# Feed-forward stages of a two-block transformer kernel: 54 pairs of output tiles as seven half-size products, down projection in three parts

## The chip, the cores and the metric

The kernel runs on one core of a Trainium2 chip. The metric is the device time in microseconds (us) of one execution; lower is better. The time before is the median of three runs.

## The reference, cut to what matters

Two blocks of two layers each act on a sequence of 512 rows and 1024 columns, all in float32. Each of the four layers ends in a feed-forward stage with 2816 inner columns. In the first block (layers 0 and 1 here):

```python
h2 = modulate(rms_norm(x, norm2_g), shift2, scale2)
u, g = jnp.split(h2 @ w_up, 2, axis=-1)
u = causal_dwconv(u, w_conv, b_conv)      # 3 taps along the sequence
y = (jax.nn.silu(u) * g) @ w_down
x = x + gate2[:, None, :] * y
```

In the second block (layers 2 and 3 here):

```python
h = rmsnorm(x, norm_ffn[i])
g = h @ w_gate; u = h @ w_up
x = x + (silu(g) * u) @ w_down
```

## The kernel before, in words

All activations lie transposed: columns of the model on the 128 partitions, the 512 rows of the sequence along the free dimension. X is the residual stream in eight such tiles. Every operand of a matmul is held as two float32r parts, high and low (HH and HL for the normed input, FH and FL for the inner activations, hi and lo for weights), and a product of a 128x128 weight block with a 128x512 activation is three matmuls: high with high, high with low, low with high (lines 440 to 442, function dot).

**Weights.** SyncE loads chunks of 512 KB (eight blocks of 128x128) into a ring of six slots, raw. The load of chunk n waits until chunk n-6 has been used up; the waits stand in one queue, in the order of the chunks (sync_program). ScalarE rounds a chunk into hi (line 1371, split), up to four chunks ahead of TensorE, at fixed places of its own program; GpSimd subtracts and writes lo (line 2977, pool_program), in the order of the chunks. VectorE and ScalarE each run one list of steps in order; what stands behind a waiting step waits too.

**A feed-forward stage.** ffn_up computes, for each f of 22, one output tile "up" and one "gateup" (projects, project, tile_of), each eight blocks deep: 24 matmuls 512 columns wide. Output goes to one of four PSUM banks in turn. In layers 0 and 1, ScalarE evicts "up" with the last tap of the convolution (line 1860), VectorE adds the other two taps (2672, 2675), ScalarE applies silu (1863). In layers 2 and 3 VectorE scales by the row roots RW (2665), then silu (1853). When "gateup" is done VectorE multiplies (2655), in layers 2 and 3 scales by RW again (2658), ScalarE writes FH (1849) and VectorE FL (2660). After all 22 tiles, out_proj multiplies FH and FL, 22 blocks deep, by the down weights, for eight tiles d, and VectorE adds them to X (x_update, 2120 and 2122). Some of the last tiles d are done in two halves of 256 rows of the sequence (WHOLE is the number of those done whole), so that the next norm can begin on the first half.

**What is woven in.** In layer 0 the products that make the modulation vectors (ada) are woven between the tiles: at each step that is not BUSY the schedule puts in a piece. Their weights come through the same ring of six slots, and VectorE multiplies and adds them (2291, 2294, 2317, 2321).

## Time and profile before

| | us |
|---|---|
| median of 3 runs | 2902.85 |
| lowest and highest run | 2902.02, 2904.55 |
| span of the profiled execution | 2901.7 |
| TensorE busy, share of the span | 2866.5, 99% |
| VectorE, ScalarE, GpSimd busy | 1115.5, 1075.3, 1171.4 |

The span goes from the first to the last instruction of one execution; the profile has no total for that execution, so its own time is taken as its span, 1.15 us under the median of the runs. In rows of the timeline the first number is the start in us from the span's start, the second the duration; the bracket says how long the engine had been idle and who released it. In rows of the groups, the numbers behind the bar are the busy time in us and the mean duration in ns, then the idle time before them.

### The profile page before, as it was taken

How to read it: one execution, taken by the hardware profiler on the slowest of the kernel's cores; microseconds unless marked ns; L12 is line 12 of the kernel's file. 1: busy time of each engine (PE TensorE's matmuls, PEld its weight loads, DVE VectorE, ACT ScalarE, POOL GpSimd, SP SyncE). 2: the span in 40 equal slices, each digit the busy share in tenths (PEclk: the TensorE clock that was granted, in tenths of full speed). 3: DMA queues.
4: the chain of work that ended last, by engine and by line, in shares of the span. 5: the costliest groups of instructions: out<-in, count | busy, mean ns of one | idle time of the engine just before them, and what ended most of it. 6: DMA issues, size and time to landing. Idle time of an engine off the chain costs nothing.

```text
span 2901.7 us, 33894 instructions
## 1 busy us (share of the span) xinstructions
PE 2866.5 (99%) x14219; PEld 2354.9 (81%) x14219; DVE 1115.5 (38%) x1787; ACT 1075.3 (37%) x1627; POOL 1171.4 (40%) x499
## 2 busy tenths in 40 slices
PE   8999999999999999999999999999999999999999
PEld 5777888888888887788898888888888877788888
DVE  6444572466664534322242211532221256622211
ACT  4335333343332434532343332342222366432322
POOL 2332245344444432344444444444444423344442
PEclk9999999999999999999999999999999999999999
DMA  8331353346554421333333333333333322233332
GB/s 257 103 106 51 106 189 114 90 153 196 195 194 136 115 73 44 88 94 96 101 88 101 95 95 94 96 97 98 94 98 95 105 60 72 77 97 95 98 95 77
DMA packets 507276, 314.04 MB, mean 108 GB/s; under 512 B 14290, under 2 KB 478836, under 8 KB 506868
## 3 DMA queue, kind: packets, MB, share of 16 engines
q1 hardware_dynamic: 507124, 311.87, 36.0%
q8 instruction: 113, 1.85, 0.3%
q14 instruction: 39, 0.32, 0.0%
HBM read 309.73 MB, written 2.10 MB: 107 GB/s over the span
## 4 chain that ended last, share of the span: by engine, by line
PE 95%; DVE 2%; ACT 1%; SPq 1%; DMA 1%; issue 0%; POOL 0%; DVEq 0%; ACTq 0%
PE b L440 22%; PE b L442 21%; PE b L441 21%; PE o L440 6%; PE o L442 6%; PE o L441 6%; PE s L769 1%; DVE aP L2834 1%; PE o L923 1%; PE b L1109 1%; PE b L1111 1%; PE b L1110 1%; PE s L903 1%; PE b L491 0%; PE b L492 0%; PE b L493 0%
## 5 line engine op out<-in xcount | busy, mean ns | idle before, releaser
L2977 POOL TENSOR_TENSOR lo<-raw,hi 128x1024 fp32r<-128x1024 f32 (+2 forms) x489 | 1169.1, 2398 | 1695.8 <-ACT hi L1371 1695.7
L440 PE MATMUL b<-HH,hi 128*128 128x512 f32 x1832 | 726.2, 396 | 1.7 <-DVE X L2120 0.9
L442 PE MATMUL b<-HH,lo 128*128 128x512 f32 x1832 | 713.7, 390 | 0.0
L441 PE MATMUL b<-HL,hi 128*128 128x512 f32 x1832 | 713.6, 390 | 0.0
L1371 ACT ACTIVATE hi<-raw 128x1024 fp32r<-128x1024 f32 (+2 forms) x492 | 506.5, 1035 | 366.8 <-DMA raw<-in_w_down_dram 96.8
L440 PEld LDWEIGHTS b<-HH,hi 128*128 128x128 f32 x1832 | 343.9, 188 | 81.4 <-issue 8.4
L442 PEld LDWEIGHTS b<-HH,lo 128*128 128x128 f32 x1832 | 343.9, 188 | 72.8
L441 PEld LDWEIGHTS b<-HL,hi 128*128 128x128 f32 x1832 | 344.1, 188 | 71.2 <-issue 1.4
L440 PE MATMUL b<-FH,hi 128*128 128x512 f32 (+1 forms) x550 | 207.2, 377 | 0.0
L442 PE MATMUL b<-FH,lo 128*128 128x512 f32 (+1 forms) x550 | 207.0, 376 | 0.0
L441 PE MATMUL b<-FL,hi 128*128 128x512 f32 (+1 forms) x550 | 207.0, 376 | 0.0
L440 PE MATMUL o<-HH,hi 128*128 128x512 f32 x520 | 202.4, 389 | 0.0
L441 PE MATMUL o<-HL,hi 128*128 128x512 f32 x520 | 202.3, 389 | 0.0
L442 PE MATMUL o<-HH,lo 128*128 128x512 f32 x520 | 202.3, 389 | 0.0
L2655 DVE TENSOR_TENSOR CB<-CB,b 128x512 f32<-128x512 f32 x84 | 57.7, 687 | 290.4 <-PE b L442 287.3
L1849 ACT ACTIVATE FH<-CB 128x512 fp32r<-128x512 f32 x88 | 55.6, 632 | 268.1 <-DVE CB L2658 199.2
L2294 DVE SCALAR_TENSOR_TENSOR AA<-raw,CA,AA 128x512 f32<-128x512 f32 x140 | 136.3, 974 | 4.1
L440 PEld LDWEIGHTS b<-FH,hi 128*128 128x128 f32 x550 | 103.5, 188 | 19.0
L441 PEld LDWEIGHTS b<-FL,hi 128*128 128x128 f32 x550 | 103.5, 188 | 18.9
L442 PEld LDWEIGHTS b<-FH,lo 128*128 128x128 f32 x550 | 103.5, 188 | 18.7
L441 PEld LDWEIGHTS o<-HL,hi 128*128 128x128 f32 x520 | 97.6, 188 | 20.3
L442 PEld LDWEIGHTS o<-HH,lo 128*128 128x128 f32 x520 | 97.6, 188 | 20.2
(517 smaller groups left out, 4012.5 us busy)
## 6 DMA issues: line engine op xcount, KB each, us to landing
raw<-in_w_up_dram SPq DMA_DIRECT2D x88, 512.0 KB, 3.9
raw<-in_w_ada_dram SPq DMA_DIRECT2D x80, 512.0 KB, 4.8
raw<-in_w_in_dram SPq DMA_DIRECT2D x76, 512.0 KB, 4.0
raw<-in_w_mg_dram SPq DMA_DIRECT2D x48, 512.0 KB, 3.7
raw<-in_ffn_w_gate_dram SPq DMA_DIRECT2D x44, 512.0 KB, 3.8
raw<-in_ffn_w_up_dram SPq DMA_DIRECT2D x44, 512.0 KB, 3.9
raw<-in_w_down_dram SPq DMA_DIRECT2D x32, 512.0 KB, 3.7
raw<-in_ffn_w_down_dram SPq DMA_DIRECT2D x32, 512.0 KB, 3.6
```

What stands on the lines that cost most here:

```text
L440: e.matmul(out, wh, xh, start=start and k == 0, stop=False)
L441: e.matmul(out, wh, xl, start=False, stop=False)
L442: mm = e.matmul(out, wl, xh, start=False, stop=stop and k == last)
L769: e.matmul(bank[b][:, 0:w], t["rk"][:, h, j * 128:j * 128 + 128], t["rq"][:, h, j * 128:S], start=True, stop=True).then_inc(*m.attn.up(("r ...
L903: e.matmul(o[:, 0:w], t["fq"][:, h, i * 128:w], t["fk"][:, h, 0:w], start=True, stop=False)
L923: mm = e.matmul(bank["o"][:, j * 128:S], t["fv"][:, j, h * 128:h * 128 + 128], t["foxT"][:, c0:c0 + S - 128 * j], start=(j == 0), stop=(j ...
L1109: e.matmul(out[:, :], hi[:, k, :], AH[:, k, :], start=(i == 0), stop=False)
L1371: e.activation(t["hi"][:, c % NSLOT, 0:w], K.raw[:, c % NSLOT, 0:w], ACT.Copy).then_inc(*m.hi.up(c))
L1849: e.activation(t["FH"][:, f, :], CB[:, b, :], ACT.Copy).then_inc(*m.atake.up(("fh", i, f)))
L2294: a = e.scalar_tensor_tensor(out=AA[:, :], in0=raw[:, k * 512:k * 512 + 512], scalar=CA[:, kk:kk + 1], in1=AA[:, :], op0=ALU.mult, op1=ALU ...
L2655: e.tensor_tensor(CB[:, b, :], CB[:, b, :], self.out_of(key)[:, :], ALU.mult).then_inc(*m.vtake.up(key))
L2977: e.tensor_tensor(t["lo"][:, s, 0:w], K.raw[:, s, 0:w], t["hi"][:, s, 0:w].bitcast(F32), ALU.subtract).then_inc(*m.lo.up(n))
```

## The change

For 54 pairs of tiles ("up" f and "gateup" f) the two tiles of eight blocks are computed as seven products of four blocks' depth on 256 columns, after Strassen, in the form with eight sums ahead (Winograd's). 6 pairs are in layer 0 and 16 in each other layer; DIRECT names the f that stay as they were. Per layer, four operands T are made once from HH and HL by twelve VectorE operations of 1024 columns (halves_whole, halves_sums, halves_low) and four of ScalarE (halves_high), in the first four f (HEAD). Per pair, VectorE makes four sums of weight quarters from the raw chunks: sum31 (1024 columns, two sums), sum2 (512, in place in raw), sum4 (512); ScalarE rounds them (pair_high: e31, the chunk nb, e4) and VectorE makes the low parts of e31 (1024) and e4 (512). The low parts of the two chunks na and nb stay with GpSimd; that of na now also waits for sum4. This is done while the tile or pair before is computed. After the products VectorE combines: pair_out row 0 is two operations of 512 columns, row 1 is one more, from copies MP that ScalarE takes of two products in the middle of the pair (pair_copies); two of the seven products overwrite or add to what was copied, and wait for it.

The down projection is done in three parts: blocks 0 to 6 after f = 7, 7 to 13 after f = 14, 14 to 21 at the end by out_proj. FH and FL have eight tiles instead of 22, and VectorE adds to X after each part (down_update, 512 columns). The banks of this stage are six instead of four. In layer 0's and the last layer's down projection WHOLE goes from 7 to 5.

The diff, cut to its core; left out are the names of the new areas, the moved bodies of the tile steps (the same operations under new names ffn_tap, ffn_conv, ffn_silu, ffn_gate, ffn_high, ffn_low) and the rest of the twelve operations for T:

```diff
 BUSY = "busy"
-WHOLE = (8, 5, 7, 5, 8, 8, 8, 8, 7)
...
 BIG4 = ["b0", "b1", "b2", "o"]
+BIG6 = ["b0", "b1", "b2", "o", "s0", "s1"]
+DIRECT = ((*range(9), 10, 11, 13, 14, 15, 17, 19), (0, 1, 2, 3, 11, 18), (0, 1, 2, 3, 11, 18), (0, 1, 2, 3, 11, 18))
+HEAD = 4
+ROOM = 8
+DOWN = {7: (0, 7), 14: (7, 7)}
+LAST = 14
+def ffn_next(i, f):
+    return f + 1 if f + 1 < KF and f + 1 not in DIRECT[i] else None
...
+        self.order = BIG6
+        for f in range(HEAD, KF):
+            if f in DIRECT[i]:
+                for key, ap, c0, freed in jobs(f):
+                    yield from self.project(ap, c0, key, freed)
+            else:
+                yield from self.pair(i, f, up_freed)
+            if f in DOWN:
+                yield from self.down(i, wd, *DOWN[f])
+        self.order = BIG4
+    def half_product(self, out, W, X, start, waits, keys):
+        e, m = self.e, self.m
+        self.q.wait_ge(*waits)
+        (wh, wl), (xh, xl) = W, X
+        for k in range(4):
+            c = slice(128 * k, 128 * k + 128)
+            e.matmul(out, wh[:, c], xh[:, k, :], start=start and k == 0, stop=False, skip_group_check=True)
+            e.matmul(out, wh[:, c], xl[:, k, :], start=False, stop=False, skip_group_check=True)
+            mm = e.matmul(out, wl[:, c], xh[:, k, :], start=False, stop=k == 3, skip_group_check=True)
+        if keys:
+            mm.then_inc(*m.dense.up(*keys))
+    def pair(self, i, f, up_freed):
...
+        K.chunks[na]["above"] = K.chunks[nb]["below"] = (i, f)
+        sa, sb = na % NSLOT, nb % NSLOT
+        hi, lo = t["hi"], t["lo"]
+        EH, EL, _ = K.block(i, f)
+        A11, A12 = [(hi[:, sa, c], lo[:, sa, c]) for c in (slice(0, 512), slice(512, 1024))]
+        s2, A22 = [(hi[:, sb, c], lo[:, sb, c]) for c in (slice(0, 512), slice(512, 1024))]
+        s3, s1, s4 = [(EH[:, u, :], EL[:, u, :]) for u in (*K.ends(na), 2)]
+        T1, T3, T2, T4 = [(t["TH"][:, j, :, :], t["TL"][:, j, :, :]) for j in range(4)]
...
+        bc_, ba, bd = [self.take_bank((x, i, f)) for x in ("up", "mid", "gateup")]
+        C, A, G = self.bank[bc_], self.bank[ba], self.bank[bd]
+        self.half_product(C[:, left], A12, H(1, left), True, [m.lo.at(na), self.free[bc_]], [])
+        self.half_product(A[:, right], s3, T3, True, [m.vtake.at("e31", i, f), m.vtake.at("t", i, 1), self.free[ba]], [])
+        yield BUSY
+        self.half_product(A[:, left], A11, H(0, left), True, [], [("mid", i, f)])
+        self.half_product(G[:, right], s1, T1, True, [m.vtake.at("t", i, 0), self.free[bd]], [("mid5", i, f)])
+        yield BUSY
+        self.half_product(C[:, right], s4, H(1, right), True, [m.vtake.at("e4", i, f)], [("block", i, f)])
+        self.half_product(A[:, left], s2, T2, False, [m.lo.at(nb), m.vtake.at("t", i, 2), m.atake.at("mid", i, f)],
+                          [("up", i, f)])
+        yield BUSY
+        self.half_product(G[:, left], A22, T4, True, [m.vtake.at("t", i, 3), m.atake.at("mid5", i, f)],
+                          [("gateup", i, f), ("chunk", na), ("chunk", nb)])
+        yield BUSY
...
+            if c in K.chunks and K.chunks[c]["split"] and "below" not in K.chunks[c]:
                 w = K.chunks[c]["width"]
...
+    def pair_high(self, i, f, part):
+        EH, _, ER = K.block(i, f)
+        if part == 0:
+            q.wait_ge(m.vtake.at("sum31", i, f))
+            e.activation(EH[:, 0:2, :], ER[:, 0:2, :], ACT.Copy).then_inc(*m.atake.up(("e31", i, f)))
+        elif part == 1:
+            q.wait_ge(m.vtake.at("sum2", i, f))
+            s = (na + 1) % NSLOT
+            e.activation(t["hi"][:, s, :], K.raw[:, s, :], ACT.Copy).then_inc(*m.hi.up(na + 1 if K.pairs else ("b", i, f)))
+        else:
+            q.wait_ge(m.vtake.at("sum4", i, f))
+            e.activation(EH[:, 2, :], ER[:, 2, :], ACT.Copy).then_inc(*m.atake.up(("e4", i, f)))
+    def pair_copies(self, i, f):
+        e, q, m, t, K = self.e, self.q, self.m, self.t, self.K
+        A, G = [self.bank[K.where.get((x, i, f), "b0")] for x in ("mid", "gateup")]
+        g = pair_before(i, f, 1)
+        q.wait_ge(m.dense.at("mid", i, f), m.vnorm.at("h", ffn_norm(i), 1, 7), m.anorm.at("sd", ffn_norm(i), 1),
+                  m.vtake.at("out2", i, g) if g is not None else None)
+        e.activation(t["MP"][:, 0:3:2, :], A[:, :].rearrange("p (h c) -> p h c", h=2), ACT.Copy,
+                     scale=-1.0).then_inc(*m.atake.up(("mid", i, f)))
+        q.wait_ge(m.dense.at("mid5", i, f))
+        e.activation(t["MP"][:, 1, :], G[:, 256:512], ACT.Copy).then_inc(*m.atake.up(("mid5", i, f)))
...
+                self.split(n + AHEAD - 1)
+                if late is not None:
+                    self.ffn_tap(i, late, self.m.vtake.at("out1", i, late))
+                prepare(g, (0, 1))
+                yield BUSY
+                if late is not None:
+                    self.ffn_silu(i, late)
+                prepare(g, (2,))
+                yield BUSY
+                self.pair_copies(i, f)
+                if late is not None:
+                    self.ffn_high(i, late)
+                yield BUSY
+                self.split(n + AHEAD)
+                yield BUSY
+                late = f
+            if f in DOWN or f == KF - 1:
+                if late is not None:
+                    self.ffn_tap(i, late, self.m.vtake.at("out1", i, late))
+                    self.ffn_silu(i, late)
+                    self.ffn_high(i, late)
...
+    def pair_sums(self, i, f):
...
+        e.tensor_tensor(ER[:, 0:2, :], ends, A21.rearrange("p (o c) -> p o c", o=1).to_broadcast([128, 2, 512]),
+                        ALU.add).then_inc(*m.vtake.up(("sum31", i, f)))
+        q.wait_ge(m.vtake.at("sum31", i, f))
+        e.tensor_tensor(A21, s1, A11, ALU.add).then_inc(*m.vtake.up(("sum2", i, f)))
+        q.wait_ge(m.vtake.at("sum2", i, f))
+        e.tensor_tensor(ER[:, 2, :], A12, A21, ALU.add).then_inc(*m.vtake.up(("sum4", i, f)))
...
+    def pair_low(self, i, f, part):
+        EH, EL, ER = K.block(i, f)
+        if part == 0:
+            q.wait_ge(m.atake.at("e31", i, f), m.vtake.at("sum4", i, f))
+            e.tensor_tensor(EL[:, 0:2, :], ER[:, 0:2, :], EH[:, 0:2, :].bitcast(F32), ALU.subtract).then_inc(
+                *m.vtake.up(("e31", i, f)))
+        else:
+            q.wait_ge(m.atake.at("e4", i, f))
+            e.tensor_tensor(EL[:, 2, :], ER[:, 2, :], EH[:, 2, :].bitcast(F32), ALU.subtract).then_inc(
...
+        A, MP = self.out_of(("mid", i, f)), t["MP"]
+        if row == 0:
+            q.wait_ge(m.dense.at("up", i, f), m.atake.at("mid", i, f), m.atake.at("mid5", i, f))
+            e.tensor_tensor(MP[:, 1:3, :], MP[:, 1:3, :],
+                            A[:, 0:256].rearrange("p (o c) -> p o c", o=1).to_broadcast([128, 2, 256]),
+                            ALU.subtract).then_inc(*m.vtake.up(("mid", i, f)))
+            q.wait_ge(m.vtake.at("mid", i, f))
...
+        def prepare(g, j):
+            if g is not None and j % 2 == 0:
+                self.pair_sums(i, g)
+                self.pair_low(i, g, 0)
+            elif g is not None:
+                self.pair_low(i, g, 2)
+        def take(j):
+            self.ffn_jobs(i, j)
+            if j == 2:
+                self.halves_whole(i)
+            if j == 3:
+                self.halves_sums(i)
+            if j in (4, 5):
+                self.halves_low(i, (2 * j - 8, 2 * j - 7))
+            if j >= 2 * HEAD - 2:
+                prepare(ffn_next(i, j // 2), j)
+        gate = self.t["MOD"][:, i, 40:48] if i < 2 else None
+        yield from self.projects(range(2 * HEAD), ffn_norm(i), take)
+        late = None
+        for f in range(HEAD, KF):
...
+            else:
+                self.next_chunk()
+                self.next_chunk()
+                if g is not None:
+                    self.pair_sums(i, g)
+                yield BUSY
+                if late is not None:
+                    self.pair_out(i, late, 1)
+                    self.ffn_conv(i, late)
+                if g is not None:
+                    self.pair_low(i, g, 0)
+                yield BUSY
+                if late is not None:
+                    self.ffn_gate(i, late)
+                    self.ffn_low(i, late)
+                if g is not None:
+                    self.pair_low(i, g, 2)
+                yield BUSY
+                self.pair_out(i, f, 0)
+                yield BUSY
+                late = f
+            if f in DOWN or f == KF - 1:
+                late_tile(late)
+                late = None
...
+                    yield from self.tile(3)
+                    self.down_update(i, k0, d, gate)
+                    if d >= KD - 2:
+                        prepare(ffn_next(i, f), d)
...
-        q.wait_ge(m.hi.at(n))
+        q.wait_ge(m.hi.at(n), m.vtake.at("sum4", *chunk["above"]) if "above" in chunk else None)
         e.tensor_tensor(t["lo"][:, s, 0:w], K.raw[:, s, 0:w], t["hi"][:, s, 0:w].bitcast(F32), ALU.subtract).then_inc(
             *m.lo.up(n))
```

## Rows read from the trace of the kernel before

**Rows 1.** The page's busy times: us (share of the span) xinstructions.

```profile
PE 2866.5 (99%) x14219; PEld 2354.9 (81%) x14219; DVE 1115.5 (38%) x1787; ACT 1075.3 (37%) x1627; POOL 1171.4 (40%) x499
```

**Rows 2.** The page's chain that ended last.

```profile
PE 95%; DVE 2%; ACT 1%; SPq 1%; DMA 1%; issue 0%; POOL 0%; DVEq 0%; ACTq 0%
```

**Rows 3.** Busy time by stretch: tiles of layers 0 and 2.

```profile
core 0: us, PE busy (x) PEld busy (x) DVE busy (x) ACT busy (x) POOL busy (x), PEclk, DMA share, GB/s
595.00:816.00 221.00, 221.00 (x989) 182.48 (x989) 139.77 (x184) 84.34 (x103) 95.29 (x40) 1.00 0.58 188
...
1978.00:2175.00 197.00, 197.00 (x871) 163.13 (x870) 50.87 (x74) 56.73 (x72) 85.80 (x36) 1.00 0.33 96
```

**Rows 4.** Timeline, PE, first matmul of two tiles in a row, 24 matmuls apart.

```profile
1961.43 0.39 PE L440 MATMUL b<-HH,hi 128*128 128x512 f32 x1
...
1966.87 0.39 PE L440 MATMUL o<-HH,hi 128*128 128x512 f32 x1
```

**Rows 5.** Timeline, PE, 256 columns: two matmuls that are 30 apart.

```profile
572.10 0.28 PE L442 MATMUL b<-MH,lo 128*128 128x256 f32 x1
...
575.70 0.28 PE L493 MATMUL b<-HH,lo 128*128 128x256 f32 x1
```

**Rows 6.** Timeline, DVE, one f of layer 2.

```profile
1961.63 0.69 DVE L2665 TENSOR_TENSOR CB<-b,RW 128x512 f32<-128x512 f32 x1 [2.63 <-PE b L442]
1967.07 0.69 DVE L2655 TENSOR_TENSOR CB<-CB,b 128x512 f32<-128x512 f32 x1 [4.75 <-PE b L442]
1967.79 0.69 DVE L2658 TENSOR_TENSOR CB<-CB,RW 128x512 f32<-128x512 f32 x1
1969.18 0.69 DVE L2660 TENSOR_TENSOR FL<-CB,FH 128x512 fp32r<-128x512 f32 x1 [0.70 <-ACT FH L1849]
```

**Rows 7.** One source line, DVE: the only operation with 1024 columns.

```profile
L2247 DVE TENSOR_TENSOR lo<-raw,hi x3: 1216/1224/1225, 20.2 to 22.9; 128x1024 fp32r<-128x1024 f32 x3
```

**Rows 8.** Timeline, ACT: FH and the next chunk's hi, layer 2.

```profile
1968.51 0.63 ACT L1849 ACTIVATE FH<-CB 128x512 fp32r<-128x512 f32 x1 [4.58 <-DVE CB L2658]
1969.05 1.04 ACT L1371 ACTIVATE hi<-raw 128x1024 fp32r<-128x1024 f32 x1
```

**Rows 9.** Timeline, DVE and ACT, layer 1: tap and convolution.

```profile
1511.43 0.78 ACT L1860 ACTIVATE CB<-o,PAR 128x512 f32<-128x512 f32 x1 [3.13 <-PE o L442]
...
1512.24 0.75 DVE L2672 SCALAR_TENSOR_TENSOR CB<-o,PAR,CB 128x511 f32<-128x511 f32 x1 [4.17 <-ACT CB L1860]
1513.03 0.75 DVE L2675 SCALAR_TENSOR_TENSOR CB<-o,PAR,CB 128x510 f32<-128x510 f32 x1
```

**Rows 10.** Groups by form, all POOL.

```profile
L2977 POOL TENSOR_TENSOR lo<-raw,hi 128x1024 fp32r<-128x1024 f32 x451 | 1100.1, 2444 | 1669.6 <-ACT hi L1371 1669.4
```

**Rows 11.** Timeline: a DVE operation that starts while POOL is at work.

```profile
598.82 2.39 POOL L2977 TENSOR_TENSOR lo<-raw,hi 128x1024 fp32r<-128x1024 f32 x1 [4.96 <-ACT hi L1371]
...
599.29 2.46 DVE L2660 TENSOR_TENSOR FL<-CB,FH 128x512 fp32r<-128x512 f32 x1 [0.71 <-ACT FH L1849]
```

**Rows 12.** Timeline, start of layer 1's stage: DVE, POOL.

```profile
1494.09 0.75 DVE L2672 SCALAR_TENSOR_TENSOR CB<-o,PAR,CB 128x511 f32<-128x511 f32 x1
...
1497.32 9.94 POOL L2977 TENSOR_TENSOR lo<-raw,hi 128x1024 fp32r<-128x1024 f32 x4 [4.96 <-ACT hi L1371]
```

**Rows 13.** Timeline, start of layer 2's stage: DVE, POOL.

```profile
1950.75 0.69 DVE L2665 TENSOR_TENSOR CB<-o,RW 128x512 f32<-128x512 f32 x1 [2.63 <-PE o L442]
...
1953.13 2.40 POOL L2977 TENSOR_TENSOR lo<-raw,hi 128x1024 fp32r<-128x1024 f32 x1 [2.32 <-ACT hi L1371]
```

**Rows 14.** Busy time by stretch, at the start of the kernel.

```profile
16.00:19.00 3.00, 0.00 (x0) 0.00 (x0) 2.90 (x5) 2.53 (x5) 0.00 (x0) 1.00 1.07 323
...
21.00:23.00 2.00, 2.00 (x11) 0.86 (x11) 1.80 (x4) 1.33 (x3) 0.00 (x0) 0.50 1.08 352
```

**Rows 15.** Groups of ACT and DVE in layer 0's tiles, 595 to 816 us.

```profile
L1371 ACT ACTIVATE hi<-raw 128x1024 fp32r<-128x1024 f32 x40 | 42.4, 1060 | 69.8 <-DMA raw<-in_w_up_dram 66.8 <-DMA raw<-in_w_down_dram 3.0
...
L2294 DVE SCALAR_TENSOR_TENSOR AA<-raw,CA,AA 128x512 f32<-128x512 f32 x69 | 51.8, 750 | 1.4
```

More of the change, by code:

```diff
@@ L34 @@
 BUSY = "busy"
-WHOLE = (8, 5, 7, 5, 8, 8, 8, 8, 7)
+WHOLE = (8, 5, 5, 5, 8, 8, 8, 8, 5)
 BIG3 = ["b0", "b1", "b2"]
@@ L38, with pair_before, pair_block @@
 BIG4 = ["b0", "b1", "b2", "o"]
+BIG6 = ["b0", "b1", "b2", "o", "s0", "s1"]
[6 more added lines that the diff above has]
+    return f + 1 if f + 1 < KF and f + 1 not in DIRECT[i] else None
+def pair_before(i, f, n):
+    pairs = [g for g in range(KF) if g not in DIRECT[i]]
+    j = pairs.index(f) - n
+    return pairs[j] if j >= 0 else None
+def pair_block(i, f):
+    return [g for g in range(KF) if g not in DIRECT[i]].index(f) % 2
 def tables():
```

314 lines of the change are left out of this document (238 added, 76 removed).

## The prediction, made before the changed kernel had run

> **What bounds the kernel now.** I read the page's busy times first: TensorE is busy for 99% of the span, every other engine for 37 to 40% [rows 1]. The chain that ended last is 95% TensorE [rows 2]. So this is a kernel of one long stream of matmuls; other engines count only where they make that stream wait. Then the stretches of feed-forward tiles: TensorE has no idle time in them; VectorE is busy for 139.8 of 221.0 us in layer 0, with the modulation's work woven in, and for 50.9 of 197.0 us in layer 2; GpSimd for 43% in both [rows 3]. The clock is full there.
>
> **What the products give back.** One tile of 24 matmuls of 512 columns takes 1966.87 - 1961.43 = 5.44 us, 0.2267 us a matmul [rows 4]. With 256 columns, 30 matmuls take 3.60 us, 0.120 us each [rows 5]. A pair of tiles is now 48 wide matmuls, 10.88 us; as seven products it is 7 x 4 x 3 = 84 narrow ones, 10.08 us. An eighth of the columns goes, but narrow matmuls are dearer per column, so a pair gives 0.80 us and 54 pairs 43.2 us, if TensorE never waits. (The Trainium skill, TensorE: Matmul & The Clock Gate, Back-to-back issue gap, gives N/2.4 + 2.5 ns, which is 215.8 and 109.2 ns; by it a pair would give 1.19 us and 54 pairs 64 us. The rows of this kernel disagree with it, most for 256 columns, and I go by them.)
>
> **What it costs the other engines.** A VectorE operation of 512 columns takes 0.69 us, and the dependent next one starts 0.72 after it [rows 6]; one of 1024 takes 1.22 [rows 7]. A pair adds two of 1024 and six of 512: 2 x 1.22 + 6 x 0.69 = 6.6 us. The old work of an f is four of 0.69 and the wait of 0.70 for FH, 3.5 us [rows 6]; with the convolution 0.1 us more [rows 9]. That is 10.1 us, some 10.4 with the gaps, against 10.08 us of TensorE. ScalarE adds 1.04 for e31, 0.63 for e4 and some 1.1 for the two copies [rows 8]: about 7 us, room enough. GpSimd keeps two operations of 2.40 [rows 10].
>
> But VectorE and GpSimd do not overlap freely. FL, which reads two SBUF tensors, started 0.47 us into a GpSimd operation, and took 2.46 us instead of 0.69; it ended 0.54 after GpSimd did [rows 11]. Of the pair's eight new VectorE operations five read two SBUF tensors (three sums, two low parts), and of the old ones FL and, in layers 2 and 3, the second scaling. The three of pair_out read PSUM and are free, as line 2655 is.
>
> **One pair in a run**, from the start S of sum31. Layers 2, 3: sums end S+2.7; GpSimd starts lo(na), ends S+5.15; VectorE meanwhile does pair_out row 1 and scaled, then e31's low part is held to S+6.25; lo(nb) runs to S+8.65; the second scaling is held to S+9.2; FH 0.7, FL, e4's low part, pair_out row 0: S+12.8. In layers 0, 1 there is no second scaling, and FL is held instead: S+11.35. Both exceed 10.08, so VectorE loses 2.7 or 1.3 us per pair in a run. ScalarE's pair_copies stands behind e4's rounding, so behind the sums: the first copy ends at S+4.5, with a late f S+6 (S+7 in layers 0, 1). TensorE needs it 7.2 us (60 matmuls) into the pair. I call the pair's unhindered start p.
>
> **The waits that follow**
> - A pair behind a direct f, layers 2, 3. "Up" is done 0.2 after its tile; scaled, sums 2.7, e31's low part; GpSimd does lo(na) behind it until p+1.8. "Gateup" is only done at p+0.2: multiply, second scaling (held), FH, FL (held by lo(nb), p+4.8), e4: S = p+6.0. Copy p+10.5 against p+7.2: 3.3 us. Two per layer, 13.2. Layer 1, with tap and convolution [rows 9]: 4.2 each, 8.4. In layer 0 four pairs stand alone and need only lo(na), at p+3.5; with the fifth, 17.5.
> - A pair behind a part of the down projection. Its sums wait for the last tile but one, which leaves 4.76 us (21 matmuls) for 0.9 + 2.7 + 1.25 + 2.40 = 7.25: 2.5 us, six times, 15.0.
> - Third pair of the run 4 to 7: S = p+3.3 and a late f: 2.0 in layers 2 and 3, some 2 in all in layer 1; 6.
> - The twelve operations for T, 12 x 1.25 = 15 us, in the first four f. Layer 2: from scaled 1 [rows 13] and one GpSimd operation of 2.4 in between, the list runs whole 1958.6, f 1 and sums 1966.5, f 2 and low 1975, scaled 3, sums of pair 4 1978.4, e4 1986.3. The pair was due at 1977.7, so S = p+8.6: 5.9 us, in layer 3 too, 11.8. Layer 1 starts later and meets two GpSimd operations [rows 12]: the same list from 1494.1 ends at 1535 against p = 1516.6: S = p+18.3, 15.6 us. In layer 0 the pair comes at f = 9, and the lag has five f to shrink, beside modulation work that leaves VectorE 37% idle [rows 3]: between 0 and 15, I take 5.
>
> Sum of waits: 13.2 + 8.4 + 17.5 + 15.0 + 6 + 11.8 + 15.6 + 5 = 92.5. A restart after a wait isn't in it: nothing to 0.2 us each, some 25 times. After 3 us without a matmul the granted clock is 0.50 for the rows behind [rows 14]: after the three long waits a few us at 1.2 GHz, up to 6 in all.
>
> **Costed at nothing.** The down projection has the same 22 x 24 wide matmuls; its narrow ones go from 66 pairs of halves to 72, 0.08 us in two layers. 64 more additions to X (0.69 to 0.75 us) lie beside tiles of 4.76 us; if that cover went, 46 us. Loads keep number and bytes; SyncE's queue gets a pair's two slots at once, three pairs ahead, some 20 us of cover. Six banks leave eviction more room than four. At the end of a stage the late tile 21 has seven blocks of three tiles, 14 us, before its FH is read; its own steps take 5 to 9.
>
> **Sum.** 2901.7 - 43.2 + 92.5 = 2951.0 for the profiled execution; the median stands 1.15 above its span: **2952 us**, slower by 1.7%. Its own range, with layer 0's lag, restarts and clock and the waits a fifth less or more, is 2925 to 2980.
>
> **The rivals.**
> 1. *TensorE stays the bound, faster.* If the preparation gets ahead, so that behind a direct f S is p+2.7 or less, the copies come in time and only the starts of the layers and the down parts wait, some 15 us: 2902.85 - 43 + 15 = 2875 us. For it: the totals per layer fit, as VectorE has down parts of 38 us to rest. Against: the preparation of a pair cannot start before the tile ahead is evicted, and the order within VectorE's list is fixed. 22%.
> 2. *GpSimd holds nobody.* If VectorE's operations fall between GpSimd's, as most of FL's do in layer 2 [rows 6], the waits are 1.1 x 4 + 2.2 x 7 + 1.35 x 6 + 2 x 2 + 9.3 = 41, and the gain is eaten without a loss: 2902.85 - 43.2 + 41 = 2901. Against: lo(na) is released by sum4, in the middle of VectorE's list. 10%.
> 3. *Layer 0's ring dries up, much slower.* VectorE behind by 15 us uses up modulation chunks late; the SyncE queue waits for their slots, with the weights behind them; ScalarE already waits 66.8 us for such loads here [rows 15]. VectorE's busy 139.8 plus 15 for T, 39.5 for six pairs, more holding, in 216 us: it decides when VectorE has no idle time left before f = 9. Another 15 to 45 us: 2980. 18%.
> The forecast has the other 50%.
>
> **Chances.** About 0.2% is what a measurement of this kernel can tell from no change. Faster: rival 1, 0.22. Within 0.2%: most of rival 2, 0.08. Slower: 0.70. The range of 8 in 10 runs from inside rival 1 to inside rival 3: 2872 to 2992.
>
> **What would show it.** Right: 84 narrow matmuls at 0.120 apart; TensorE's idle time in the groups is some 90 us, released by lo (first product), e4's low part and ScalarE's copies MP; VectorE's two-SBUF operations have medians well over 0.69 and 1.22; the first pair of layer 1 starts late by over 10 us. TensorE's busy time falls by some 40. Rival 1: the same fall, and idle time under 40 us. Rival 3: ScalarE waits for DMA of w_up by far more than 67 us in layer 0. Wrong altogether would be a spacing of the narrow matmuls other than 0.120, or sums of weight quarters that take longer than plain operations.

## The result, and the profile after

The changed kernel takes **3059.36 us** (median of 4 runs, 3052.16 to 3063.21), against 2902.62 us for the kernel before on the same chip: ratio 1.0533, 95% interval 1.052 to 1.0545. The forecast was 2952 us in a range of 2872 to 2992: slower, as forecast, but by 157 us instead of 49, and outside the range. The profiled execution spans 3057.9 us, 156.2 more than the one before.

The page's busy times and the chain that ended last, which answer to [rows 1, 2]:

```profile
PE 2884.2 (94%) x16175; PEld 2455.8 (80%) x16175; DVE 1785.0 (58%) x2339; ACT 1212.5 (40%) x1865; POOL 1250.5 (41%) x499
...
PE 69%; DVE 16%; ACT 5%; DMA 4%; issue 3%; POOL 2%; SPq 1%; DVEq 0%; POOLq 0%; ACTq 0%
```

TensorE is no longer nearly the whole chain: 31% of it now runs through others, against 5% before. Its waits, from the view of who waited for what (engine, line and tile waited for; us in total, times, longest):

```profile
PE s L1223 <- POOL lo L3379: 40.7, 12, 13.1
PE b L1223 <- ACT MP L2035: 23.5, 18, 2.2
PE b L1223 <- POOL lo L3379: 18.8, 8, 3.1
PE s L1223 <- ACT MP L2035: 17.9, 12, 2.6
PE o L1223 <- ACT MP L2035: 15.5, 9, 2.2
```

Two waits of the new products carry the loss. 20 times the first product of a run of pairs waits for GpSimd's low part (59.5 us idle), and 39 times the sixth product of a pair waits for ScalarE's copy MP of the third (56.9 us). Of these 39, 34 are in pairs that follow another pair: every such pair has this wait, 0.46 to 2.35 us over the usual distance of two matmuls. Behind the waits comes the clock, in the busy times of the four feed-forward stages and of two short stretches behind a wait; [rows 3] had 1.00:

```profile
core 0: us, PE busy (x) PEld busy (x) DVE busy (x) ACT busy (x) POOL busy (x), PEclk, DMA share, GB/s
571.00:985.00 414.00, 377.52 (x1990) 324.12 (x1988) 305.34 (x356) 144.85 (x193) 171.98 (x67) 0.96 0.51 152
1528.00:1937.00 409.00, 365.23 (x2249) 332.50 (x2248) 273.40 (x291) 167.43 (x234) 183.60 (x69) 0.95 0.30 86
2034.00:2426.00 392.00, 364.17 (x2193) 326.92 (x2193) 272.58 (x272) 149.21 (x206) 183.22 (x69) 0.98 0.32 90
2660.00:3048.00 388.00, 362.22 (x2258) 328.61 (x2256) 263.18 (x268) 144.94 (x204) 170.92 (x65) 0.98 0.29 83
...
1587.50:1589.00 1.50, 1.50 (x7) 1.50 (x8) 1.50 (x2) 0.46 (x1) 1.50 (x1) 0.50 0.00 0
1609.30:1611.50 2.20, 2.20 (x11) 2.20 (x12) 1.60 (x2) 0.57 (x2) 1.29 (x1) 0.50 0.00 0
```

VectorE is busy for 70% of layer 2's stage (272.58 of 392.00 us), where it was busy for 21% before (77.26 of 361.00).

An account of the 156 us. I took, for every matmul behind 560 us, the distance of its start from the start before it, less the usual distance (0.227 us wide, 0.120 narrow). What is over 150 ns, and makes twice the usual or more, I call a gap; what is near 0.21 us for a narrow one, the half clock.

| us | before | after |
|---|---|---|
| gaps that MP ended | | 63.1 |
| gaps at the first product of a run, ended by lo | | 62.7 |
| half clock in the narrow products of pairs | | 37.4 |
| half clock in wide ones | 11.9 | 18.6 |
| all gaps outside the pairs, most of them of wide products | 15.2 | 40.4 |
| saved by 54 pairs | | -43.2 |

63.1 + 62.7 + 37.4 + 6.7 + 25.2 - 43.2 = 151.9, and 3.1 us of other gaps in pairs: 155.0 of 156.2.

By stage (from the last update of X ahead of it to its own last one, in the trace), the feed-forward of layers 0 to 3 went from 366.5, 361.1, 360.5, 363.9 us to 413.7, 408.4, 386.5, 386.8, and the stretch between layers 0 and 1 from 532.0 to 543.9: modulation work left over, whose last AA operation starts at 986.4 instead of 894.5.

**How a copy comes late.** The timeline of ScalarE in layer 1 (start, duration, operation, in brackets the idle time before it and what ended it):

```profile
1595.55 0.38 ACT L2038 ACTIVATE MP<-b 128x256 f32<-128x256 f32 x1 [0.60 <-PE b L1225]
1603.93 1.06 ACT L1501 ACTIVATE hi<-raw 128x1024 fp32r<-128x1024 f32 x1 [8.00 <-DMA raw<-in_w_up_dram]
1604.90 0.76 ACT L1981 ACTIVATE CB<-s,PAR 128x512 f32<-128x512 f32 x1
1605.56 1.05 ACT L2019 ACTIVATE EH<-ER 128x1024 fp32r<-128x1024 f32 x1
1606.51 1.04 ACT L2023 ACTIVATE hi<-raw 128x1024 fp32r<-128x1024 f32 x1
1607.45 0.62 ACT L1988 ACTIVATE CB<-CB 128x512 f32<-128x512 f32 x1
1607.97 0.62 ACT L2026 ACTIVATE EH<-ER 128x512 fp32r<-128x512 f32 x1
1608.49 0.58 ACT L2035 ACTIVATE MP<-o 128x512 f32<-128x512 f32 x1
1608.97 0.38 ACT L2038 ACTIVATE MP<-s 128x256 f32<-128x256 f32 x1
```

and of SyncE's queue and TensorE around it:

```profile
1599.87 0.99 SPq L3405 DMA_DIRECT2D raw<-in_w_up_dram  x2
...
1606.75 0.28 PE L1225 MATMUL b<-HH,EL 128*128 128x256 f32 x1
1609.22 0.55 PE L1223 MATMUL o<-TH,hi 128*128 128x256 f32 x1 [2.19 <-ACT MP L2035]
```

The pair before ended at 1599.55 and freed both its slots at once; the load into them was issued at 1599.87 and landed at 1603.9. ScalarE had stood in front of it since 1595.93, since its list copies the high part of the chunk **two pairs ahead** first; the tap, e31, hi, silu and e4 follow, and only then the copy, for which TensorE had been waiting since 1606.87.

### The profile page after: what moved, and what is told of

It reads as the page before. It is cut to its first block, busy times and chain, and to the rows that moved or that the text cites. A ratio compares the mean times of both kernels' runs of the same rounds, so it can differ in the third digit from the quotient of the medians.

```text
span 3057.9 us, 38722 instructions
## 1 busy us (share of the span) xinstructions
PE 2884.2 (94%) x16175; PEld 2455.8 (80%) x16175; DVE 1785.0 (58%) x2339; ACT 1212.5 (40%) x1865; POOL 1250.5 (41%) x499
## 4 chain that ended last, share of the span: by engine, by line
PE 69%; DVE 16%; ACT 5%; DMA 4%; issue 3%; POOL 2%; SPq 1%; DVEq 0%; POOLq 0%; ACTq 0%
PE b L494 12%; PE b L496 12%; PE b L495 12%; PE o L494 3%; PE o L496 3%; PE o L495 3%; POOL lo L3379 2%; DMA raw<-in_w_down_dram 2%; PE b L1223 2%; DVE EL L2978 2%; PE s L494 2%; PE s L495 2%; PE s L496 2%; PE b L1224 2%; PE b L1225 2%
## 5 line engine op out<-in xcount | busy, mean ns | idle before, releaser
L1501 ACT ACTIVATE hi<-raw 128x1024 fp32r<-128x1024 f32 (+1 forms) x438 | 449.9, 1034 | 533.1 <-DMA raw<-in_w_down_dram 128.5
L494 PE MATMUL b<-HH,hi 128*128 128x512 f32 x1048 | 422.5, 403 | 7.5 <-POOL lo L3379 5.8
L496 PE MATMUL b<-HH,lo 128*128 128x512 f32 x1048 | 409.7, 391 | 0.0
L495 PE MATMUL b<-HL,hi 128*128 128x512 f32 x1048 | 409.6, 391 | 0.0
L494 PEld LDWEIGHTS b<-HH,hi 128*128 128x128 f32 x1048 | 197.4, 188 | 57.0 <-POOL lo L3379 8.7
L496 PEld LDWEIGHTS b<-HH,lo 128*128 128x128 f32 x1048 | 197.3, 188 | 42.6
L495 PEld LDWEIGHTS b<-HL,hi 128*128 128x128 f32 x1048 | 197.7, 189 | 40.7 <-issue 1.4
L2911 DVE TENSOR_TENSOR FL<-CB,FH 128x512 fp32r<-128x512 f32 x88 | 96.4, 1096 | 63.2 <-ACT FH L1995 63.2
L2978 DVE TENSOR_TENSOR EL<-ER,EH 128x512 fp32r<-128x512 f32 x54 | 117.8, 2181 | 0.0
L2974 DVE TENSOR_TENSOR EL<-ER,EH 128x1024 fp32r<-128x1024 f32 x54 | 109.9, 2035 | 8.5 <-ACT EH L2019 4.7
```

What stands on the lines that cost most here:

```text
L494: e.matmul(out, wh, xh, start=start and k == 0, stop=False)
L495: e.matmul(out, wh, xl, start=False, stop=False)
L496: mm = e.matmul(out, wl, xh, start=False, stop=stop and k == last)
L1501: e.activation(t["hi"][:, c % NSLOT, 0:w], K.raw[:, c % NSLOT, 0:w], ACT.Copy).then_inc(*m.hi.up(c))
L2911: e.tensor_tensor(t["FL"][:, f % ROOM, :], t["CB"][:, f % 2, :], t["FH"][:, f % ROOM, :].bitcast(F32), ALU.subtract).then_inc(*m.vtake.up( ...
L2974: e.tensor_tensor(EL[:, 0:2, :], ER[:, 0:2, :], EH[:, 0:2, :].bitcast(F32), ALU.subtract).then_inc(*m.vtake.up(("e31", i, f)))
```

## The experiments

Lines move by up to 17 between these kernels. A run's ratio is to the kernel before on its chip; the intervals are 0.1 to 0.2% to either side, so that a difference of two runs is known to some 4 to 6 us.

**1 to 3. Load or place in the list.** Run 1 frees the slot early:

```diff
-        self.half_product(A[:, left], A11, H(0, left), True, [], [("mid", i, f)])
+        self.half_product(A[:, left], A11, H(0, left), True, [], [("mid", i, f), ("chunk", na)])
...
-                          [("gateup", i, f), ("chunk", na), ("chunk", nb)])
+                          [("gateup", i, f), ("chunk", nb)])
```

Run 2 moves the high part to a later place, and run 3 does both:

```diff
                 n = self.next_chunk()
-                self.split(n + AHEAD - 1)
```

> Edit: a pair frees its upper chunk's slot at the third of its seven block products, the last that reads this slot, and no longer at the seventh. Theory A (ScalarE's list): at the head of a pair ScalarE copies the high part of the chunk two pairs ahead, whose slot came free only at the end of the pair before, so that it waits 7 to 8 us for the load (hi at 1617.64 in the changed kernel waited 7.77), and the copies that TensorE needs stand behind it. The load then starts some 5.8 us sooner, the wait mostly goes, most of the 63.1 us of gaps released by the middle copies and part of the 37.4 us lost to the half clock in narrow products go too: 2970 to 3005 us. Rival B (VectorE and GpSimd are too full; the sums and low parts of each pair are late by themselves): less than 25 us, 3035 to 3060. Rival C (the load is late because the DMA queue is behind, not because of the slot): no change, 3050 to 3062.

> Edit: at the head of a pair ScalarE no longer copies the high part of the chunk two pairs ahead; it does so after the pair's own copies. Slots come free as late as before. Theory A: what holds TensorE is the place in ScalarE's list and not the load as such, so the middle copies are no longer late: most of the 63.1 us of gaps goes, 2970 to 3010 us, and if this gives about as much as freeing the slot early, it is the order that matters. Rival B (VectorE and GpSimd are too full): less than 25 us, 3035 to 3060. Rival D (the later high part makes GpSimd's low part of that chunk late, so that the wait only moves to the head of the next pair): 3020 to 3060 and more gaps released by GpSimd's low part.

> Edit: both, the upper chunk's slot freed at the third block product and the high part two pairs ahead copied after the pair's own copies. Theory A: the two take away the same wait, so together they give little more than the better of the two alone: 2960 to 3000 us, the gaps released by the middle copies under 10 us in all (63.1 before). Rival B: 3035 to 3060. If the two gains add up to their sum, theory A is wrong in that they are one wait.

Measured: 3038.75 us, 3012.78 us and 3012.61 us (ratios 1.0463, 1.0378, 1.0374). Copies' gaps went from 63.1 to 46.9, 28.1 and 31.1 us, half clock in narrow products from 37.4 to 26.7, 25.6 and 23.9. The two are one wait: alone they give 20.6 and 46.6 us, together 46.8. The place in the list is the cause; the slot only decides how long the wait is. But all three times lie above theory A's ranges (run 1 in that of rival B), and with both edits 31.1 us of these gaps are left where it had allowed under 10: they had another origin.

**4, 5. The rest of the change without pairs.** Every f in DIRECT; in 5 also no halves_whole, halves_sums, halves_low, halves_high.

> Edit: every f is computed directly, none as seven half-size products; the down projection in three parts, the TH, TL and TR operations of each layer and everything else stay. Before had 2902 us. Theory: the 54 pairs carry nearly all of the loss, against what they save (0.80 us of TensorE each, 43 us); the three parts cost TensorE only a few short waits and the T operations delay nobody much, since no first pair waits for them: 2903 to 2925 us. Rival E (the down projection in three parts and the T operations cost much by themselves, by their updates on VectorE and the smaller F ring of 8): over 2940 us.

> Edit: no pairs, and the sums, high and low parts of the blocks of H (TR, TH, TL) left out too; only the down projection in three parts and the F ring of 8 are left of the change. With them it was 2920.1 us, and layer 0 alone was 12.9 us longer than before, with a gap of 6.19 us at 611.31 that ended on GpSimd's low part. Theory F: the T operations stand in VectorE's list ahead of layer 1's ada work, whose slots and buffers come free later, so in layer 0 they are the loss: layer 0's feed-forward back within 4 us of before's 366.5, 2905 to 2912 us. Rival G: the loss comes from the down projection in three parts (its chunks of 448 KB take slots of the same ring, so less ada work gets done in layer 0): layer 0 still over 374 us, 2914 to 2921 us.

Measured: 2920.06 us (1.0053) and 2906.94 us (1.001, interval 1.0001 to 1.0019). So the down projection in three parts costs 2.5 us, in layer 0 (370.1 against 366.5), and the T operations some 13 us, 9.3 of them in layer 0 (379.4), where one gap of 6.19 us at 611.31 disappears with them. Everything else is the pairs'. In layer 1 the T operations cost nothing by themselves: its stage takes 361.1 us in both runs, as before.

**6. Copies first** (on top of 2):

```diff
-                prepare(g, (0, 1))
+                self.pair_copies(i, f, 0)
+                prepare(g, (0,))
+                self.pair_copies(i, f, 1)
+                prepare(g, (1,))
...
-                self.pair_copies(i, f)
```

> Edit: as the kernel with the high part two pairs ahead copied later (3012.8 us), and ScalarE's two copies of a pair's middle products stand in its list ahead of the next pair's high parts instead of behind them. In that kernel the gaps inside pairs still grew along a run of pairs, 1.07, 1.52, 2.30 us, 28.1 us in all, and the copies ran right behind e31, hi and e4 of the next pair. Theory A2 (order of ScalarE's list again): the copies are early, under 8 us of such gaps are left, half clock in narrow products (25.6 us) falls too: 2975 to 2995 us. Rival B (VectorE needs over 10.1 us for each pair beside GpSimd, so the pair's period is set there and the gap only moves to another product, on a low part of VectorE or GpSimd): 3003 to 3015 us.

Measured: 3003.33 us (1.0339). The gaps that copies end fell from 28.1 to 4.2 us as forecast, the time by only 9.5 (14.2 between the two profiled executions): by 4.2 us the first products of runs waited longer, those outside the pairs by 2.4, and the half clock stayed. The mechanism was right, its price was not, and the time lies at the edge of rival B's range. Part of what the copies gave back went to other waits.

**7. First pair of a run prepared early** (on top of 2):

```diff
             if f in DIRECT[i]:
+                prepare(g, 0)
                 late_tile(late)
                 late = None
                 for j in (2 * f, 2 * f + 1):
                     yield from self.tile()
+                    if j % 2:
+                        prepare(g, 1)
                     self.ffn_jobs(i, j)
-                    prepare(g, j)
```

and the same in ScalarE's list, and one tile earlier behind a down part.

> Edit: as the kernel with the high part two pairs ahead copied later (3012.8 us), and for the first pair of a run, behind a direct f or a down part, VectorE makes the sums and ScalarE the high parts ahead of the direct tile's own operations (one tile earlier behind a down part). Theory H: the 62.0 us of gaps at the first product of a run, released by GpSimd's low part, come from the place of the sums in VectorE's list; those behind a direct f (3.5 us in layers 0 and 1, 1.87 in layers 2 and 3) and behind a down part (2.5 to 2.6) go, which are 13 of the 20 gaps and 35 us; the four first pairs of the layers stay (13.5 us in layer 1). 2975 to 2990 us. Rival I: the loads of this pair's chunks come no earlier, or the direct tile's own results become late: under 10 us gained, over 3002 us.

Measured: 2981.77 us (1.0264), 31.0 less. Of 20 gaps with 62.0 us 8 with 39.3 are left: the first pairs of layers 1 to 3, among them the one of 13.5, and all five of layer 0. In layers 1 to 3 the twelve gaps behind a direct f or a down part are gone: there VectorE's place for the sums was the cause. In layer 0 theory H was wrong and rival I right: sum31 now waits for the load of w_up before each of the five pairs (24.6 us in all), and their gaps grew from 16.2 to 20.7 us, the last two to 6.5 and 7.0.

**8. All three, layer 0 direct, layer 1 from f 6.**

> Edit: high part two pairs ahead later, copies first, first pair of a run prepared early, no pairs and no T operations in layer 0, and layer 1's pairs begin at f 6 and not at f 4 (46 pairs stay). Theory: each of the waits named is taken away and what the pairs save shows: 46 x 0.80 is 36.8 us less of TensorE, against some 12 us for layer 0 with its down projection in three parts or 3 without T operations, 2 x 2.9 us at the first pairs of layers 2 and 3, and what stays at the half clock: 2885 to 2925 us. Rival B (VectorE and GpSimd hold the pairs by their mere load): over 2935 us.

Measured: 2914.17 us (1.0033), inside the expected range: six of the fifteen runs of pairs now go without a wait, three pairs in 30.23 us, 10.08 each, which is 84 x 0.120. VectorE's load alone does not hold three pairs that start well prepared. Behind a direct f the second pair still waits 1.6 to 2.0 us.

**9. Layer 0 alone put back:**

```diff
-DIRECT = ((*range(9), 10, 11, 13, 14, 15, 17, 19), (0, 1, 2, 3, 11, 18), (0, 1, 2, 3, 11, 18), (0, 1, 2, 3, 11, 18))
+DIRECT = (tuple(range(22)), (0, 1, 2, 3, 11, 18), (0, 1, 2, 3, 11, 18), (0, 1, 2, 3, 11, 18))
...
-            if j == 3:
+            if j == 3 and i:
...
```

> Edit: the changed kernel (3059.4 us) with layer 0 alone put back: no pairs and no T operations there; the other three layers and all lists as changed. Theory J: the six pairs of layer 0 and its T operations cost what the stages say: 413.7 against 370.1 us for the feed-forward with neither, and 543.9 against 532.6 between this layer and the next, because ada work is crowded out of layer 0 and done behind it: 55 us less, 2995 to 3012 us, and the 13.5 us before the first pair of layer 1 get shorter only if they come from left-over ada work. Rival: the stages hide each other's waits, so that under 40 us come back, over 3019 us.

Measured: 3012.56 us (1.0373), 46.8 less where theory J had 55, and at the edge of its range; the two stretches give back 44.4 and 11.2 us, and layer 2's became 5.9 longer. The 13.53 us gap stays, so it isn't layer 0's left-over work. Six pairs, worth 4.8 us, cost with their T operations nearly a third of the whole loss.

**10. out2 first, fewer pairs** (on top of 8): pair_out(i, late, 1) moves ahead of pair_sums(i, g) in VectorE's list, and

```diff
-DIRECT = (tuple(range(22)), (0, 1, 2, 3, 4, 5, 11, 18), (0, 1, 2, 3, 11, 18), (0, 1, 2, 3, 11, 18))
+DIRECT = (tuple(range(22)), (*range(8), 11, 18, 21), (*range(5), 11, 18, 21), (*range(5), 11, 18, 21))
```

> Edit: as the kernel with all lists changed and layer 0 direct (2914.2 us); VectorE adds the second output of the pair before (out2) ahead of the next pair's sums, since the copies of ScalarE waited for it (8.63 us before 2003.40); the first pair is f 5 in layers 2 and 3 and f 8 in layer 1, and f 21 is direct (39 pairs stay). Theory: 3.9 us before the first pair of layer 1 and 2.9 us in layers 2 and 3 go, 5.2 us of gaps behind the copies go, and most of the 4.2, 2.3 and 1.3 us ahead of the last part go, against 7 pairs fewer at 0.80 us: 2893 to 2904 us. Rival B (VectorE's load): over 2908 us.

Measured: **2892.7 us, 0.9965 of the kernel before (interval 0.9954 to 0.9977)**: the first version that beats it. Its page, and what TensorE still waits for in pairs:

```profile
PE 2842.8 (98%) x15635; PEld 2403.9 (83%) x15635; DVE 1565.8 (54%) x2207; ACT 1176.0 (41%) x1801; POOL 1222.2 (42%) x499
...
PE 84%; DVE 9%; ACT 3%; DMA 2%; POOL 1%; issue 1%; SPq 1%; DVEq 0%; POOLq 0%; ACTq 0%
```

```profile
PE b L1223 <- POOL lo L3387: 5.3, 3, 1.8
...
PE o L1223 <- POOL lo L3387: 3.6, 2, 1.8
```

TensorE is busy for 98% of the span and is 84% of the chain, against 99 and 95% in [rows 1, 2]: its work is nearly the time again. Of the 31.2 us that 39 pairs save, 11.6 show. This run changed the order and the choice of the f together; what each gave was not tried.

**11, 12. The second pair behind a direct f.** 11 puts its sums ahead of the direct f's second half on VectorE; 12 also puts the direct f's FH behind the pair's first copy on ScalarE.

> Edit: as the kernel before it in this list, and the sums of the second pair behind a direct f stand ahead of that direct f's second half in VectorE's list. In the kernel with all lists changed this second pair waited 1.6 to 2.0 us in each of six runs of pairs, 10.6 us in all, while the other runs went at 10.08 us a pair. Theory: these waits go: 8 to 14 us below the kernel without this edit, 2882 to 2895 us. Rival K: the raw chunks of this pair come too late for it and VectorE stands still in front of the gate and low part of the direct f: no gain, or up to 10 us lost.

> Edit: as the kernel with the second pair's sums early (2897.1 us), and ScalarE's high part of F of the direct f (FH, 2107.16) stands behind the first copy of the pair that follows. In that kernel GpSimd's low part no longer held the second pair, but this FH, whose data VectorE finished only at 2107.1, stood ahead of the copies at 2107.70, and TensorE waited 2.97 us at 2105.45; such gaps were 17.8 us in all. Theory (the order of ScalarE's list, a third time): the copies run some 4 us earlier, at least 10 of the 17.8 us go: 2880 to 2890 us. Rival K2 (VectorE's load around the direct f is the cause, which only picks another place each time): 2892 to 2900 us.

Measured: 2897.05 us (0.9976) and 2892.94 us (0.9962). Both theories fall by their numbers: run 11 is 4.4 us above run 10, inside rival K's "up to 10 us lost", and run 12 lies in rival K2's range. The 11.7 us of gaps that lo ended went to none, and 17.8 us ended by MP came in their place, 12.7 in run 12. The wait moves from list to list; I read it as more work behind a direct f than fits there, which no run shows by itself. In run 12 this is why FH is late (timeline of VectorE and GpSimd):

```profile
2100.94 0.69 DVE L2976 TENSOR_TENSOR ER<-raw 128x512 f32<-128x512 f32 x1
2101.55 0.68 DVE L2913 TENSOR_TENSOR CB<-CB,s 128x512 f32<-128x512 f32 x1
2102.26 2.46 DVE L2916 TENSOR_TENSOR CB<-CB,RW 128x512 f32<-128x512 f32 x1
...
2101.78 2.40 POOL L3396 TENSOR_TENSOR lo<-raw,hi 128x1024 fp32r<-128x1024 f32 x1 [7.19 <-DVE ER L2976]
```

The second scaling needs 0.69 us alone and took 2.46, from inside GpSimd's operation until 0.54 us behind its end, as in [rows 11]. That led to the next pair of runs.

**13, 14. GpSimd's operation for pairs with one input**, in the changed kernel and in version 10:

```diff
+        if "above" in chunk or "below" in chunk:
+            e.tensor_copy(t["lo"][:, s, 0:w], K.raw[:, s, 0:w]).then_inc(*m.lo.up(n))
+        else:
...
```

Both kernels leave out the low parts of the pairs' weights: a copy of the whole chunk stands in their place, so what they compute is not the product, and only their time is of use.

> Edit: in the changed kernel (3059.4 us) GpSimd's operation for the two chunks of each pair reads one input instead of two: it copies the raw chunk and does not subtract the high part (so the low parts of these weights are left out of the computation; sizes, waits and everything else stay). It was 2.4 us long, 3.4 beside VectorE. Theory L (the lock matters little, the lists do): the operation gets shorter or at least VectorE's operations beside it no longer last until its end, but TensorE gains only where VectorE or GpSimd released it: the first pairs of runs (62.7 us, of which perhaps a quarter), so 3030 to 3055 us. Rival M (the lock is the main cause: some 7 us in each pair's lists): over 60 us gained, under 3000 us. If a copy locks VectorE as before and is as long, nothing changes and the run tells only that.

> Edit: the same in the best version so far (2892.7 us): GpSimd copies the raw chunk of a pair and does not subtract the high part (the low parts of these weights are left out of the computation). There 11.7 us of gaps released by GpSimd's low part and some 5 us at the half clock in narrow products are left. Theory L: with shorter shared time the sums of the second pair behind a direct f come earlier, 5 to 14 us gained: 2878 to 2888 us. Rival: the sums stand behind the direct f's own results and not behind locked operations, so under 3 us are gained.

Measured: 2997.11 us (1.0321), 62.3 less, and 2876.64 us (0.9902), 16.1 less. Groups of the changed kernel, then of run 13 (count, busy time, mean ns, idle time before and its releaser):

```profile
L2978 DVE TENSOR_TENSOR EL<-ER,EH 128x512 fp32r<-128x512 f32 x54 | 117.8, 2181 | 0.0
L2974 DVE TENSOR_TENSOR EL<-ER,EH 128x1024 fp32r<-128x1024 f32 x54 | 109.9, 2035 | 8.5 <-ACT EH L2019 4.7
```

```profile
L3380 POOL CAST lo<-raw 128x1024 fp32r<-128x1024 f32 x108 | 158.7, 1488 | 564.7 <-DVE ER L2965 501.9 <-ACT hi L2023 62.8
L2974 DVE TENSOR_TENSOR EL<-ER,EH 128x1024 fp32r<-128x1024 f32 x54 | 78.9, 1461 | 29.8 <-ACT EH L2019 26.0
...
L2978 DVE TENSOR_TENSOR EL<-ER,EH 128x512 fp32r<-128x512 f32 x54 | 60.7, 1123 | 0.0
```

In the changed kernel rival M's number came true and theory L's didn't; in version 10 the gain is 2 us above theory L's range. GpSimd's operation for pairs, by its length or by what it holds up on VectorE, is a main cause. Gaps at the first products fell from 62.7 to 35.9, those at copies from 63.1 to 48.5, and the half clock in narrow products from 37.4 to 15.4. In layer 2, where the second scaling is held as well, the stage fell by 23.1 us, in layer 1 by 9.0. In run 14 all fourteen runs of pairs go at 10.08 us a pair: no gap and no half clock in them. The copy is shorter alone (1.04 us at best, 2.40 for the subtraction), and is itself up to 2.10 us long beside VectorE. It still holds VectorE: in run 13 the 512-column low part has a mean of 1.12 us, against 0.69 where it stands alone. So these runs shorten the shared time and don't take it away. How much of the gain is the lock and how much the shorter operation, these runs don't tell apart.

**15. Layer 1 from f 8**, in the changed kernel: DIRECT[1] = (*range(8), 11, 18).

> Edit: the changed kernel (3059.4 us) with f 4 to 7 of layer 1 direct, so that its first pair is f 8, behind the first down part. The gap of 13.5 us stayed when layer 0 was direct (13.53 us at 1518.92), so left-over work of layer 0 does not make it. Theory N: it is the T operations and the sums of f 4 behind the layer's first tiles, and with the first pair 50 us later they are long done: 13.5 us go, and with the four pairs the waits of their run (2.5, 2.4, 1.3 us and the half clock behind them), less 4 x 0.80 us of TensorE: 3059 - 13.5 - 6 to 10 + 3.2, so 3035 to 3045 us. Rival: T operations in layer 1 delay the wide products as well, or the gap moves to f 8: under 8 us gained.

Measured: 3058.6 us (1.0532), no gain: the rival's number. The gap moved to the wide products of a direct f, 6.71 us at 1580.97, where TensorE waited for a bank that VectorE had not read, and the runs behind became no better. VectorE's list before that point, and the matmul that waited:

```profile
1554.64 9.02 DVE L2926 TENSOR_TENSOR TR<-HH,HL 128x1024 f32<-128x1024 f32 x4
...
1574.83 2.55 DVE L2946 TENSOR_TENSOR TL<-TR,TH 128x1024 fp32r<-128x1024 f32 x2
...
1580.12 4.52 DVE L2946 TENSOR_TENSOR TL<-TR,TH 128x1024 fp32r<-128x1024 f32 x2
1584.56 0.74 DVE L2891 SCALAR_TENSOR_TENSOR CB<-o,PAR,CB 128x511 f32<-128x511 f32 x1
...
1587.69 0.76 PE L494 MATMUL b<-HH,hi 128*128 128x512 f32 x1 [6.32 <-DVE CB L2902]
```

Four operations of 1.22 us took 9.02, and the tile that TensorE had finished by 1575.8 was read only at 1586.85. But the T operations alone don't make the gap: in run 4 and in version 10, whose layer 1 also begins with direct tiles (stages of 361.1 and 358.1 us), they are as long at the same place (9.02, 2.6 and 4.6 us), and TensorE has no gap. The rows show another difference, the banks. The list changes from four banks to six behind f 3, and the banks are taken by a count that runs on. In run 15 the tile at 1587.69 gets the bank of the tile at 1570.3, two tiles before; in run 4 and in version 10 the same tile gets one last used four tiles before. The six pairs of layer 0 take three banks each instead of two, which moves the count. So late reads and an early reuse of the bank meet in run 15; this is read from the rows, and no run changed the order of the banks alone. For the pair at f 4 of the changed kernel the rows have the sums from 1581.23 to 1583.90 us, behind the low parts of T and the taps of f 3, and its first product at 1587.50, when GpSimd's low part is done. That the T operations make those 13.5 us is argued from this order; no run took them away in front of a pair.

## Why the prediction was right in sign and wrong in size

- **What a pair saves, 0.80 us: right.** Undisturbed runs of pairs go at 10.08 us a pair.
- **The first pairs of the 20 runs: near.** They were to wait 81.5 us in all and waited some 70. In layer 0 the five gaps are 3.3 to 3.6 us (16.9 in all, forecast 17.5), behind the down parts 2.3 to 2.4 (14.0, forecast 15.0). Behind a direct f it is 2.6 in layers 2 and 3 (1.65 for lo, 0.93 for the copy; forecast 3.3) and 3.3 in layer 1 (forecast 4.2).
- **First pair of layer 1, 15.6 us: 13.3 measured** (13.5 from start to start); of layers 2 and 3, 5.9 forecast and 2.7 measured: the term was double its size. In the forecast the copy of that pair came last. In the rows its first product waits for GpSimd's low part, and nobody waits for its copy.
- **The step that failed, in the pairs that follow a pair: "SyncE's queue gets a pair's two slots at once, three pairs ahead, some 20 us of cover".** That is when the products need the chunk. ScalarE's list asks for it two pairs ahead, at the head of a pair, which is before or just as the slot comes free, and so has no cover. I put the first copy at S+4.5 or S+6 and asked only for sums ahead of it; in the rows above it comes behind an 8.00 us wait for a load. For the 34 pairs that follow another one the forecast had 6 us, for third pairs alone, and nothing for the second ones; they waited 56.6 us for copies. Runs 2 and 6 show what stood ahead of the copies: the gaps that copies end go from 63.1 to 28.1 us when the one instruction for the chunk two pairs ahead moves (46.6 us of time, with 11.8 of half clock in it), and to 4.2 when the next pair's high parts stand behind the copies too.
- **What the forecast lacked, 107 us.** 51 are these copies, 44 the clock, 20 gaps outside the pairs (25.2 against the 5 put in for layer 0's lag), and the first pairs give 11 back; 3 are small gaps in pairs.
- **VectorE's 12.8 and 11.35 us for a pair in a run, against 10.08: too dear.** The runs of pairs without a wait in version 8 and 10 have the same operations. In version 8 the sums of one pair start 9.5 and 10.7 us behind those of the pair before; with a head start three pairs go by without a lag that TensorE sees.
- **The clock, "up to 6 in all": wrong sevenfold.** 37.4 us in narrow and 6.7 more in wide products. I had allowed a fallen clock behind three long waits. It is also 0.50 behind waits like the one of 2.19 us above: 23 of the 59 waits at the first and sixth products were followed by some 1.6 us of loss at that clock, all of them gaps of 2.04 us or more. This is the largest term that the forecast lacked after the copies.
- **Rival 3 came true in size beside the forecast, not in its place.** Layer 0 and what is left over behind it cost 47.2 + 11.9 us against a forecast of 17.5 + 5 less 4.8. Its mechanism, a dry ring, is not shown: its sign was ScalarE's waits for w_up in layer 0, and they fell from 66.8 us [rows 15] to 28.4 (in layer 1 they rose from 1.4 to 62.6, with the step above). In the rows it is the single pairs (as forecast), 16.3 us of gaps of wide products, with the T operations in them (9.3 us, run 4 against run 5), some 14 us of half clock and left-over modulation work. Run 9 puts all of it at 46.8 us. How little slack the ring has there shows in run 7, where sums that ask earlier wait 24.6 us for loads.
- **The lock of VectorE and GpSimd: in the forecast, and right in kind.** EL's low part of 512 elements has a mean of 2.18 us. The Trainium skill, SBUF — State Buffer, section "SBUF: two separate sides", says of VectorE operations with two SBUF inputs and GpSimd operations that whichever starts first has the shared ports for its whole length and the other blocks. The rows agree: 2.46 us instead of 0.69 in run 12, ending 0.54 us behind GpSimd's operation.
- **Rival 1 is what the change could have been**, for 39 pairs: version 10, 2892.7 us.
- **One sign of being right failed**: TensorE's busy time was to fall by some 40 us and rose by 17.7, with 44 us of half clock in it. That the kernel would be slower was no luck: the waits of the first pairs of runs, forecast at 81.5 us and measured at some 70, exceed the 43.2 us saved by themselves.

After all, three lists without slack (ScalarE's, VectorE's at the runs' starts, the lock between VectorE and GpSimd) each held the same products, so that the gains overlap: 46.6 for run 2, 31.0 for run 7, 46.8 for run 9, 62.3 for run 13, more in sum than the loss. Run 14, in which no pair waits, is 27.6 us below the kernel before on its chip (2904.22); it leaves out the low parts of the pairs' weights and shows only what the waits are worth.

## What to carry to other kernels

When an engine's work is fed by others' lists in fixed order, ask of each instruction not when its result is needed but when its engine will stand in front of it, and what is queued behind; a ring's cover is counted from there. When work is cut into smaller products with more helpers, leave it out where the stretch has no slack (layer 0, the first tiles of a layer, the last f): 39 pairs with early preparation beat the kernel before by 11.6 us, and 54 lost 157. Count for a wait of some 2 us or more also the stretch at half clock that can follow it.

## What the runs showed of the hardware

Waits of some 2 us, not only long ones, can be followed by a granted clock of 0.50, which is 1.2 GHz (from 1609.30 to 1611.50 behind 2.19 us of idle time). In the changed kernel 28 gaps at the first and sixth products were 2.04 us or longer, over the usual distance, and 23 of them were followed by it; the other five (2.10, 2.11, twice 2.37, 3.27) weren't, and of the 31 shorter ones none was. In run 8 three gaps of 1.92 us were. In the changed kernel the half clock added 44 us to some 126 us of gaps at pairs.

And the wait between VectorE and GpSimd works both ways, and for a GpSimd operation with one input too. In run 13 GpSimd's copy, 1.04 us alone, took 2.09 where it started 0.03 us behind a VectorE subtraction of 1024 columns, and such a subtraction, 1.23 us alone, took 2.08 where it started 0.04 us behind the copy.
